# Gathered expert rows weighed and summed on TensorE through diagonal gate matrices, and the variance by a squaring pass of ScalarE

## The reference

```python
x = layer_norm(alpha * x + g2 * moe(x * (1 + sc2) + sh2), ln_g[1, 1], ln_b[1, 1])

def moe(h, ...):                      # top 2 of 8 experts
    gates = softmax(top_v)            # two gates for each token
    y = sum over the two chosen experts e of gate_e * swiglu(h, w1[e], w3[e], w2[e])

def layer_norm(x, g, b):
    mu = mean(x); var = mean(square(x - mu))
    return (x - mu) * rsqrt(var + 1e-5) * g + b
```

## Time and profile before

| | |
|---|---|
| median of 3 runs | 2442.57 us (2441.56 to 2445.93) |
| the profiled execution | 2446.07 us, its span 2444.3 us |
| mean granted clock of TensorE | 0.937 of full speed |
| PE busy | 2141.7 us (88%) |
| DVE busy | 1470.8 us (60%) |
| ACT busy | 1284.5 us (53%) |
| POOL busy | 758.5 us (31%) |

### The profile page before, as it was taken

One profiled execution on the slowest core, in us unless ns is written; L12 is line 12 of the kernel. 1 busy time (PEld: TensorE's weight loads), 2 busy tenths in 40 slices (PEclk: granted clock), 3 DMA queues, 4 the chain that ended last, 5 costly groups with the idle time before them and its releaser, 6 DMA issues.

```text
span 2444.3 us, 54596 instructions
## 1 busy us (share of the span) xinstructions
PE 2141.7 (88%) x23078; PEld 1337.8 (55%) x23078; DVE 1470.8 (60%) x1822; ACT 1284.5 (53%) x1664; POOL 758.5 (31%) x557
## 2 busy tenths in 40 slices
PE   5998987878989999999898878888969999999990
PEld 4765656755565555555765557654544444444440
DVE  3155745559362121214558666486379999999976
ACT  3443753446444242423443764466268787787862
POOL 0432115432314342423232135333123333332321
PEclk8999998888999999999999888889979999999995
DMA  9322990020212222215221000020276677980023
GB/s 277 105 81 76 298 302 11 3 56 4 72 53 72 84 82 73 86 68 162 86 89 38 1 10 3 3 57 22 97 257 207 233 266 275 332 314 35 27 104 137
DMA packets 215386, 278.46 MB, mean 114 GB/s; under 512 B 28178, under 2 KB 188798, under 8 KB 215040
## 3 DMA queue, kind: packets, MB, share of 16 engines
q1 hardware_dynamic: 203776, 243.60, 30.8%
q0 software_dynamic: 8432, 29.89, 3.3%
q10 hardware_dynamic: 2959, 1.83, 0.3%
HBM read 368.35 MB, written 29.11 MB: 163 GB/s over the span
## 4 chain that ended last, share of the span: by engine, by line
PE 52%; issue 16%; DVE 14%; POOL 7%; ACT 6%; DMA 3%; SPq 1%; POOLq 0%; DVEq 0%; ACTq 0%
PE ps L2268 50%; POOL mix L968 5%; DVE arena L1662 2%; DMA wbuf<-in_w_mod 1%; DVE mix L1670 1%; PE ps L2475 1%; DVE xT L1662 1%; DVE const L1662 1%; ACT arena L1142 1%; DVE mix L1662 1%; DVE mix L1666 1%; DVE yg L1662 1%; DVE arena L1666 1%; DVE hT L1662 1%; POOL mix L971 1%
## 5 line engine op out<-in xcount | busy, mean ns | idle before, releaser
L2268 PE MATMUL ps<-hT,mix 128*128 128x512 f16 (+2 forms) x3024 | 377.5, 287 | 24.7 <-DVE hT L1662 15.3
L2268 PE MATMUL ps<-w,xgT 128*128 128x512 f16 x1632 | 365.4, 381 | 7.0 <-DVE w L2163 7.0
L2163 DVE SCALAR_TENSOR_TENSOR w<-wst,w 128x2048 f16<-128x2048 f32 x136 | 309.8, 2317 | 22.8 <-ACT w L1523 22.6
L2268 PEld LDWEIGHTS ps<-hT,mix 128*128 128x128 f16 x3024 | 228.2, 99 | 172.4 <-issue 17.1
L1000 POOL TENSOR_TENSOR a<-aval,a 128x256 f16<-128x256 f32 x68 | 159.1, 2340 | 370.8 <-ACT a L1571 370.8
L2268 PEld LDWEIGHTS ps<-w,xgT 128*128 128x128 f16 x1632 | 157.1, 98 | 185.8 <-issue 10.2
L1523 ACT ACTIVATE w<-wst 128x2048 f16<-128x2048 f32 x136 | 251.5, 1899 | 6.6 <-DMA xs_rows<-htok,slot_i 6.5
L2268 PE MATMUL ps<-mix 128*128 128x512 f16 (+5 forms) x1856 | 204.5, 288 | 14.5 <-POOL mix L971 8.8
L2268 PE MATMUL ps<-hT,arena 128*128 128x128 f16 (+1 forms) x1440 | 201.2, 302 | 1.0 <-DVE const L1662 1.0
L2268 PE MATMUL ps<-w2m,aT 128*128 128x512 f16 x816 | 188.6, 381 | 5.6 <-DVE aT L2201 5.6
L2268 PEld LDWEIGHTS ps<-mix 128*128 128x128 f16 (+3 forms) x1856 | 121.3, 124 | 88.7 <-POOL mix L971 12.4
(11 more groups left out here) (360 smaller groups left out, 3625.0 us busy)
## 6 DMA issues: line engine op xcount, KB each, us to landing
wst<-in_moe_w SPq DMA_DIRECT2D x204, 1024.0 KB
wbuf<-in_w_mod SPq DMA_DIRECT2D x40, 1024.0 KB
wbuf<-in_ffn_w SPq DMA_DIRECT2D x33, 1024.0 KB
wbuf<-in_w_in SPq DMA_DIRECT2D x20, 1024.0 KB
xs_rows<-in_table SPq DMA_DIRECT2D x17, 512.0 KB, 6.3
ys_rows<-yb POOLq DMA_DIRECT2D x17, 512.0 KB, 4.0
wbuf<-in_w_out SPq DMA_DIRECT2D x32, 256.0 KB
xg<-xs_rows POOLq DMA_DIRECT2D x16, 512.0 KB, 5.7
```

What stands on the lines that cost most here:

```text
L2163: v_.scalar_tensor_tensor(out=q[1], in0=staged(s, p), scalar=WS, in1=q[0], op0=ALU.mult, op1=ALU.subtract).then_inc(sg["m_lo13"], 1)
L2268: return mm_(o, w, x, start=first, stop=last, skip_group_check=True)
```

## The change

ACT makes, ahead of the tail, ten matrices `dg[:, t, i]` of 128x128, each the identity with its rows scaled by the gates of a token tile (in the room of `xT`, which is free by then). PE multiplies each gathered tile by its matrix, two matrices into one PSUM region, and so weighs and sums the two experts' rows: four float32 products over 512 columns for a tile, into PSUM slots 0 and 1 in turn. DVE reads the sum from PSUM as it multiplies by g2. The instruction that adds the residual also puts out the sum of its result (`accum_out`), which a small `ts` turns into -mean. ACT squares (x - mean) in one pass, with the sum of squares put out, and makes the root. DVE multiplies (x - mean) by ln_g while ACT does so (`scale`), and after it multiplies by 1/sqrt(var + eps) and adds ln_b in one instruction (`shift`).

```diff
+        dg = over("dg", [P, TT, 2, P], ADDR["xT"])
...
-            def weigh(t):
-                act.wait_ge(yg_in[t], 32)
-                a.activation(yg[:, 0, t, :], yg[:, 0, t, :], ACT.Identity, scale=tq[:, 1, t:t + 1]).then_inc(sg["mix_ready"], 1)
-
-            def standard(t):
+            for t in range(TT):
+                for i in range(2):
+                    L.do(a.activation(dg[:, t, i], ident, ACT.Copy, scale=tq[:, 1 + i, t:t + 1]), "dg_ready" if i else None)
+            for t in range(TT):
+                st = lnst[:, t]
                 act.wait_ge(sg["lnv_ready"], t + 1)
-                st = lnst[:, t]
-                L.do(a.activation(st[:, 14:15], st[:, 13:14], ACT.Ln, bias=eps[:, 0:1]))
+                L.do(a.activation(yg[:, 1, t, :], yg[:, 0, t, :], ACT.Square, bias=st[:, 12:13], accum_out=st[:, 13:14]))
+                L.do(a.activation(st[:, 14:15], st[:, 13:14], ACT.Ln, scale=1.0 / D, bias=eps[:, 0:1]))
                 a.activation(st[:, 14:15], st[:, 14:15], ACT.Exp, scale=-0.5).then_inc(sg["lnr_ready"], 1)
-                act.wait_ge(sg["lnx_ready"], t + 1)
-                L.do(a.activation(yg[:, 0, t, :], yg[:, 0, t, :], ACT.Identity, scale=st[:, 14:15], bias=st[:, 15:16]),
-                     "xn_ready")
-
-            weigh(0)
-            weigh(1)
-            for t in range(TT):
-                standard(t)
-                if t + 2 < TT:
-                    weigh(t + 2)
...
             def combine(t):
-                y0, y1, st = yg[:, 0, t, :], yg[:, 1, t, :], lnst[:, t]
-                dve.wait_ge(sg["mix_ready"], t + 1)
-                stt(y0, y1, tq[:, 2, t:t + 1], y0, ALU.mult, ALU.add)
-                tt(y0, y0, rowg[:, 1 if t == 4 else 0, :], ALU.mult)
-                stt(y0, xr[:, t, :], ALPHA, y0, ALU.mult, ALU.add)
-                for h in range(2):
-                    L.do(v_.bn_stats(st[:, 6 * h:6 * h + 6], y0[:, 512 * h:512 * h + 512]))
-                L.do(v_.bn_aggr(st[:, 12:14], st[:, 0:12]), "lnv_ready")
-
-            def centre(t):
-                st = lnst[:, t]
+                y0, st = yg[:, 0, t, :], lnst[:, t]
+                dve.wait_ge(sg["y_psum"], t + 1)
+                tt(y0, ps[:, t % 2], rowg[:, 1 if t == 4 else 0, :], ALU.mult, to="y_mul")
+                L.do(v_.scalar_tensor_tensor(out=y0, in0=xr[:, t, :], scalar=ALPHA, in1=y0, op0=ALU.mult, op1=ALU.add,
+                                             accum_out=st[:, 12:13]))
+                ts(st[:, 12:13], st[:, 12:13], -1.0 / D, ALU.mult, to="lnv_ready")
+
+            def scale(t):
+                stt(xr[:, t, :], yg[:, 0, t, :], lnst[:, t, 12:13], rowg[:, 3, :], ALU.add, ALU.mult)
+
+            def shift(t):
                 dve.wait_ge(sg["lnr_ready"], t + 1)
-                stt(st[:, 15:16], st[:, 12:13], -1.0, st[:, 14:15], ALU.mult, ALU.mult, to="lnx_ready")
-
-            def spread(t):
-                dve.wait_ge(sg["xn_ready"], t + 1)
-                tt(yg[:, 0, t, :], yg[:, 0, t, :], rowg[:, 3, :], ALU.mult)
-                tt(yg[:, 0, t, :], yg[:, 0, t, :], rowg[:, 4, :], ALU.add, to="lnb_ready")
+                stt(yg[:, 0, t, :], xr[:, t, :], lnst[:, t, 14:15], rowg[:, 4, :], ALU.mult, ALU.add, to="lnb_ready")
 
             combine(0)
             for t in range(TT):
-                centre(t)
+                scale(t)
                 if t + 1 < TT:
                     combine(t + 1)
-                spread(t)
+                shift(t)
...
+            pe.wait_ge(sg["m_act"], MS)
+            for t in range(TT):
+                pe.wait_ge(sg["dg_ready"], t + 1)
+                pe.wait_ge(yg_in[t], 32)
+                if t >= 2:
+                    pe.wait_ge(sg["y_mul"], t - 1)
+                for h in range(2):
+                    c = slice(512 * h, 512 * h + 512)
+                    for i in range(2):
+                        ins = mm(ps[:, t % 2, c], dg[:, t, i], yg[:, i, t, c], i == 0, i == 1)
+                ins.then_inc(sg["y_psum"], 1)
```

More of the change, by code:

```diff
@@ L498, in backbone_kernel @@
             "m_hi13 m_lo13 m_hi2 m_lo2 m_xt m_xhi m_xlo m_up m_silu m_act m_ahi m_alo m_turn m_at "
-            "m_down m_yact m_ydve row_in xr_in mix_ready lnv_ready lnr_ready lnx_ready lnb_ready").split()}
+            "m_down m_yact m_ydve row_in xr_in dg_ready y_psum y_mul lnv_ready lnr_ready lnb_ready").split()}
         st_full = [sem(f"st_full{i}") for i in range(3 * MQ)]
```

## The result

| | before | changed |
|---|---|---|
| median (5 runs each) | 2442.57 us (2439.94 to 2445.93) | 2430.99 us (2427.28 to 2433.01) |
| profiled execution, span | 2446.07 us, 2444.3 us | 2431.03 us, 2429.2 us |
| last result tile read out of PSUM | 2384.96 us | 2381.68 us |
| first gather landed | 2396.64 us | 2393.38 us |
| from that landing to the end | 47.7 us | 35.8 us |

The changed kernel takes 0.995 of the time of the one before, 95% interval 0.9935 to 0.9965: faster, by 11.6 us in the medians. The two profiles differ by 15.1 us of span, but 3.3 us of that lie ahead of the tail, in a part that both kernels share. The row to compare is the last of the table: the tail itself is 11.8 us shorter, near the 11.6 us of the medians.

What follows compares the result with a forecast made beforehand. VectorE was taken to bound the tail: its work 14.7 us shorter, its start 4.5 us later, net -10.2 us, which taken from the 2442.57 us median gives 2432.4 us; range 2428.5 to 2439.5.

Steps and rivals of the forecast that it cites:

- What bounds the tail: Last 60 us: VectorE is full and sets the end, its stretch 43.2 us for five tiles before the change.
- The first tile: TensorE after the first gather's landing: half clock, full speed some 4.3 us after the start, first tile out after 5.8 us.
- DVE's tile: VectorE's work per token tile in the tail: 5.37 us of instructions, 5.55 us with gaps, 27.8 us for five tiles.
- the sum put out by the residual: Accumulated sum of DVE's residual instruction in each tile: taken as 0.20 us, like ACT's accumulator read of 0.193 us.
- the rival in which the sum is free: DVE's residual puts out its sum at no cost: 1.0 us less than forecast, 2431.4 us; counted inside the main case.
- main case: Tail set by DVE, TensorE reaching full clock during the first tile: 2432.4 us, spanning 2429 to 2436; chance 0.74.
- The last wait: Last token tile: only scale(4), 1.3 us, covers ACT's 2.0 us from mean to root, so DVE waits 0.7 us more.
- half-clock rival: TensorE stays at half clock in the tail, a tile every 6.8 us, and is the bound: 2438.7 us; chance 0.10.
- ScalarE: Ten diagonal matrices, 0.31 us each, hidden before the first gather lands; Square and Ln need no further table load.
- TensorE's weight loads: Matrix loads for TensorE's tail products: hidden behind the pass in flight, a pass 0.43 us at full clock.
- the second pass: The residual's sum costs DVE a second pass, 1.04 us more in each of five tiles: 2437.6 us; chance 0.07.
- the open weight loads: TensorE's weight loads not hidden at half clock, a tile 9.1 us: 2450.3 us, 7.7 us later than before; chance 0.04.

Runs made afterwards that it cites:

- either part alone: Against the kernel before: only TensorE's weighing and summing changed, tail 45.9 us; only the residual's sum, squaring pass and fused last passes changed, tail 37.8 us.
- kept-busy experiment: Changed kernel plus 51 unread float16 TensorE products until about the first gather's landing; landing to end 33.8 us, ratio 0.9948 to the kernel before.
- doubled products: Changed kernel with each TensorE product of the tail issued twice; landing to end 46.6 us, ratio 0.9995 to the kernel before.

## Why the prediction was right, point by point

The forecast was 2432.4 us, a gain of 10.2; measured were 2430.99 us and 11.6 (11.8 in the tail).

- *What bounds the tail.* DVE, right: with either part alone, the sum of DVE's instructions and its start gave the tail, to 0.9 us in one case and to under 0.1 in the other.
- *The first tile.* Predicted 5.8 us for TensorE, measured 5.77; half clock and then full speed 4.2 us after the start, as in the rotary products of the earlier trace rows, gate matrices as empty as theirs notwithstanding. DVE started 6.0 us after the landing. The kept-busy experiment shows the cause.
- *DVE's tile.* Predicted 5.55 us, measured 5.36. The term that was too large is the sum put out by the residual: 0.20 against 0.01 us. Five tiles make 0.95 us. So the rival in which the sum is free came nearest (2431.4 us); it lay inside the main case. The Trainium skill's sentence on halved throughput, which the prediction weighed (Vector Engine (DVE) Microarchitecture Reference, Points that are easy to get wrong), does not hold here: the residual with two float32 inputs in SBUF and a sum took 1.22 us.
- *The last wait.* Predicted 0.7 us, measured none. Here the step itself failed: it said that only scale(4) covers ACT's work for the last tile. The order of the loop is combine(4), shift(3), scale(4), shift(4), so two passes, 2.6 us, cover 1.8 us of ACT. This made 0.7 us; with the 0.95 us above, and less 0.2 us by which DVE started later than forecast, it is about 1.5 of the 1.6 us between forecast and measured tail. The two large terms erred the same way, so the forecast owes nothing to their cancelling. The same forgotten shift(3) stood against the half-clock rival, where it comes after the fifth tile: 1.3 us too few there, and 0.7 too many for the wait.
- *ScalarE.* The diagonal matrices took 0.40 us each and not 0.31 (the shape in the earlier trace rows had no scalar by partition), 4.3 us together, hidden as said under the wait for the gather. No table was loaded between Square and Ln.
- *TensorE's weight loads* stayed under the passes: 211 ns a load, on the mean, and 0.43 us a pass at full clock.

The groups of TensorE's products and of the diagonal matrices, from the changed kernel's groups by shape (busy us, mean ns, idle):

```profile
L2254 PE MATMUL ps<-yg,dg 128*128 128x512 f32 x40 | 19.7, 652 | 12.5 <-DMA yg<-ys_rows,slot_i 11.9 <-DVE yg L1653 0.6
...
L1579 ACT ACTIVATE dg<-const,rts 128x128 f32<-128x128 f32 x10 | 4.0, 401 | 0.3
```

Of the rivals, the half clock, the second pass and the open weight loads did not come. The doubled products show what a slow TensorE would have done: at a mean of 7.3 us a tile nearly the whole gain is gone. What the prediction did not tell apart is which half of the change earns the time. Its sum holds the answer (the weigh-and-add is 1.31 of the 2.9 us that a tile lost, and the late start takes most of that part back), but it was not drawn.

## What to carry to other kernels

Work handed to an idle TensorE started at half clock here: price its first piece at that speed, and if the engine can be given harmless products until the data land, the late start shrinks by what the clock cost (2.1 of 5.8 us for the first tile here). On a full VectorE count passes over the data: a statistic that rides on a pass already made (0.01 us for a sum) beats one of its own (1.63 us), and a square that a second engine can do under cover was free. An order of passes that leaves no trip over ACT open at the first and the last tile was worth 2.0 us more. Before a pass is moved from VectorE to GpSimd, look where the inputs of VectorE's other passes lie, since those with both in SBUF were held up here while GpSimd worked.

## What the runs showed of the hardware that was not expected

The sum put out by a DVE instruction cost 0.01 us beside 1.22 us. GpSimd's pass of 2.35 us held DVE's passes with two SBUF inputs that began during it until 1.1 us after its own end, and left the one with a PSUM input alone. With the last two outputs sent 1.3 us apart the end came 3.7 us after DVE's last pass, where it was 3.1 us with more time between them. And the time of the part that no kernel here changed wandered by 14 us between profiles (2376.1 to 2390.3 us to the same point), several times what most of these edits are worth.
